# Gate and q/k gain arithmetic moved between VectorE and ScalarE, and a new slot table, in a two-layer mixer and expert-retrieval kernel on one core

## What is computed

```
h = rms(x, g_mix);  x = x + mixer(h)      # 11 projected pieces of 256 columns, four mixers
h = rms(x, g_ffn);  x = x + peer(h)

mixer: qd = rms(heads(dq), g_q_dil) * 64**-0.5 ; kd = rms(heads(dk), g_k_dil)
       qs = rms(heads(bq), g_q_sb)  * 64**-0.5 ; ks = rms(heads(bk), g_k_sb)
       gating, dilated attention, short convolution, stick-breaking attention -> w_out

peer, for each token and each of 8 heads:
       s = two score vectors over 128 keys;  top 16 of each;  top 16 of the 256 sums
       g = softmax(top 16);  a = u_tab[eidx] . h ;  w = g * gelu(a)
       y += sum_k w_k * v_tab[eidx_k]
```

## Time and profile before

| | us | share of the span |
|---|---|---|
| profiled execution, device time | 3106.51 | |
| its span in the profile | 3104.7 | |
| TensorE busy | 2457.8 | 79% |
| VectorE busy | 2307.4 | 74% |
| ScalarE busy | 1421.0 | 46% |
| GpSimd busy (DMA issue) | 1237.1 | 40% |
| gathered by GpSimd's queue | 1073.81 MB | |
| moved in all | 1210.26 MB, mean 390 GB/s | |

### The profile page before, as it was taken

How to read it: one execution, slowest core, us unless ns; L and a number is a source line. 1 busy time by engine, 2 the same in 40 slices (tenths; PEclk the granted TensorE clock), 3 DMA queues, 4 the chain that set the end, 5 groups by cost and what they waited for, 6 DMA issues and landing times. The chain is left out here.

```text
span 3104.7 us, 28006 instructions
## 1 busy us (share of the span) xinstructions
PE 2457.8 (79%) x7696; PEld 1397.8 (45%) x7696; DVE 2307.4 (74%) x5378; ACT 1421.0 (46%) x3800; POOL 1237.1 (40%) x1028
## 2 busy tenths in 40 slices
PE   6579777897676887997787788897889888857666
PEld 5546354563354443663354444573445444322222
DVE  2496769568869998666867899667786899866665
ACT  2144634337643454335643455436683444533332
POOL 0133433333333344434444444334454444445443
PEclk9689889897788899999899998998899999988889
DMA  7399999899789999999999999999999999999998
GB/s 276 122 415 402 421 411 418 324 395 344 292 337 377 358 404 380 422 421 421 415 421 421 390 421 421 421 421 410 367 421 417 421 421 414 422 421 414 422 422 347
DMA packets 169787, 1210.26 MB, mean 390 GB/s; under 512 B 20896, under 2 KB 21152, under 8 KB 23200
## 3 DMA queue, kind: packets, MB, share of 16 engines
q0 software_dynamic: 147456, 1073.81, 84.6%
q1 hardware_dynamic: 22176, 134.66, 10.7%
HBM read 1206.29 MB, written 2.10 MB: 389 GB/s over the span
## 5 line engine op out<-in xcount | busy, mean ns | idle before, releaser
L462 POOL DMA_INDIRECT ring<-in_uv,idx x1024 | 1236.9, 1208 | 1844.5 <-PE psY L811 929.8
L811 PE MATMUL psY<-ring 128*128 128x512 f32 x3120 | 1579.0, 650 | 291.8 <-ACT ring L657 236.4
L1072 DVE CUSTOM_DVE_ANT_0 ring<-ring,htok 128x1024 f32<-128x1024 f32 x1024 | 1234.2, 1221 | 396.0 <-DMA ring<-in_uv,idx 382.0
L811 PEld LDWEIGHTS psY<-ring 128*128 128x128 f32 x3120 | 620.9, 208 | 1051.2 <-issue 1042.0
L647 ACT ACTIVATE gl<-adot 128x1 f32<-128x1 f32 x1024 | 205.1, 200 | 1055.0 <-DVE adot L1072 1032.3
L1083 DVE SCALAR_TENSOR_TENSOR x<-ring,wgt,x 128x1024 f32<-128x1024 f32 x244 | 312.3, 1280 | 24.0 <-issue 24.0
L684 PE MATMUL psP<-hT,wr 128*128 128x256 f32 (+1 forms) x1664 | 322.8, 351 | 3.8 <-ACT hT L499 3.1
L657 ACT ACTIVATE ring<-cst,wgt 128x128 f32<-128x128 f32 x780 | 313.3, 402 | 25.4
L688 PE MATMUL psP<-wr,hT 128*128 128x256 f32 x1344 | 308.0, 385 | 19.0 <-DMA wr<-in_w_out 13.6
L651 ACT ACTIVATE wgt<-gate,gl 128x1 f32<-128x1 f32 x1024 | 301.6, 295 | 33.3
L684 PEld LDWEIGHTS psP<-hT,wr 128*128 128x128 f32 x1664 | 283.8, 200 | 72.8 <-issue 39.3
(11 more groups left out here) (124 smaller groups left out, 1658.7 us busy)
## 6 DMA issues: line engine op xcount, KB each, us to landing
wr<-in_w_in SPq DMA_DIRECT2D x44, 1024.0 KB
wr<-in_w_q SPq DMA_DIRECT2D x40, 1024.0 KB
ring<-in_uv,idx POOLq DMA_INDIRECT x1024
wr<-in_w_out SPq DMA_DIRECT2D x16, 1024.0 KB
ring<-in_w_in SPq DMA_DIRECT2D x11, 1024.0 KB, 17.3
probs<-in_subkeys SPq DMA_DIRECT2D x5, 1024.0 KB
ring<-in_w_out SPq DMA_DIRECT2D x4, 1024.0 KB, 17.1
cat<-in_g_ffn SPq DMA_DIRECT2D x5, 512.0 KB, 12.6
```

The costliest lines, as they stand in the source:

```text
L462: pool.indirect_dma_start(out=ring[:, q % NR], out_offset=None, in_=tables[s // NC], in_offset=bass.IndirectOffsetOnAxis(ap=idx[:, s % NS, ...
L811: last = nc.tensor.matmul(psY[:, b * 512:(b + 1) * 512], ring[:, r % NR, 0:P], ring[:, r % NR, D + b * 512:D + (b + 1) * 512], start=first ...
L1072: v.tensor_tensor_reduce(out=u, in0=u, in1=htok[:, q // SLOTS % NS], scale=1.0, scalar=0.0, op0=ALU.mult, op1=ALU.add, accum_out=adot[:, J ...
```

## The change

Six edits:

- The gate: VectorE no longer subtracts the largest of the 16 (ScalarE negates it into `nmax_top` and gives it to the exponential as a bias), and no longer multiplies by 1/sum (ScalarE does at a head's first row). `top` becomes two buffers `tops`, and "top pairs" waits for the exponential of two heads earlier.
- The q/k gains: ScalarE multiplies by a gain for each partition while it takes the transposes from PSUM. VectorE multiplies q's 8 roots by 1/8 instead of the 512 values. One DMA of a [128, 4] tile takes the place of four broadcast ones.
- The parameters: two semaphores. ScalarE's hT1 waits for three small DMAs (`s_gain`), VectorE waits for the other three (`s_par`) only in the mixer parts of a layer's first step, and no longer in norm1.
- norm2: no copy to `hn`, TensorE transposes `htok`.
- No row is VectorE's in heads 6-7, 16-20, 31-36 and 47-53 (two of 16 before), so 204 rows are left to it.
- The slot table: top_rate of step 1 from 0.95 to 1.10, of (2,3) from 1.2 to 1.3, of (6,7) from 1.5 to 1.55; the three pairs start 3 slots later.

```diff
@@ -47,8 +47,7 @@
-GROUPS = [((0,), -72, 1.0, 1.0), ((1,), 22, 1.0, 0.95), ((2, 3), 126, 0.7, 1.2), ((4, 5), 336, 1.15, 1.3),
-          ((6, 7), 594, 0.97, 1.5)]
+GROUPS = [((0,), -72, 1.00, 1.00), ((1,), 22, 1.00, 1.10), ((2, 3), 129, 0.70, 1.30), ((4, 5), 339, 1.15, 1.30), ((6, 7), 597, 0.97, 1.55)]
 GROUP_LIST = [steps for steps, *_ in GROUPS]
@@ -165,11 +164,14 @@
-    return BUSY_ROWS.get(J, (3, 7, 11, 15))
-
-
-BUSY_ROWS = {J: (1, 3, 5, 7, 9, 11, 13, 15) for J in range(9, 16)}
-BUSY_ROWS.update({J: (7, 15) for lo, hi in ((6, 8), (16, 21), (31, 37), (47, 54)) for J in range(lo, hi)})
+    return BUSY_ROWS.get(J, VR)
+
+
+VR = (3, 7, 11, 15)
+VB = (1, 3, 5, 7, 9, 11, 13, 15)
+VF = ()
+BUSY_ROWS = {J: VB for J in range(9, 16)}
+BUSY_ROWS.update({J: VF for lo, hi in ((6, 8), (16, 21), (31, 37), (47, 54)) for J in range(lo, hi)})
 V_NO, _counts = {}, [0, 0]
@@ -233,7 +235,7 @@
         gain_t = sb("gain_t", [P, 2, KD])
-        g64 = sb("g64", [P, 4, HD])
+        g_col = sb("g_col", [P, 4])
         gsv = sb("gsv", [P, MW])
@@ -276,13 +278,14 @@
         si = sb("si", [P, 2, TOPK], U32)
-        top = sb("top", [P, TOPK])
+        tops = sb("tops", [P, 2, TOPK])
+        nmax_top = sb("nmax_top", [P, 1])
         pos = sb("pos", [P, 3, TOPK], U32)
...
         gsum = sb("gsum", [P, 1])
-        rsum = sb("rsum", [P, 1])
+        rsum = sb("rsum", [P, NS, PH])
         adot = sb("adot", [P, 2, TOPK])
@@ -403,10 +407,11 @@
             def parameters(l):
-                for dst, src in ((gain_t[:, 0], g_mix), (gain_t[:, 1], g_head), (sgb, b_sgu), (cvw, conv_w)):
+                for dst, src in ((gain_t[:, 0], g_mix), (gain_t[:, 1], g_head), (g_col, g_qk)):
+                    sp.dma_start(dst[:], src[l]).then_inc(s_gain, 16)
+                for dst, src in ((sgb, b_sgu), (cvw, conv_w)):
                     sp.dma_start(dst[:], src[l]).then_inc(s_par, 16)
-                for dst, g in ((g64[:, 0], g_qd), (g64[:, 1], g_kd), (g64[:, 2], g_qs), (g64[:, 3], g_ks), (gsv, g_sgu)):
-                    sp.dma_start(dst[:], g[l].partition_broadcast(P)).then_inc(s_par, 16)
+                sp.dma_start(gsv[:], g_sgu[l].partition_broadcast(P)).then_inc(s_par, 16)
@@ -444,7 +449,7 @@
-        N_PAR, N_LATE = 9 * 16, 16
+        N_GAIN, N_PAR, N_LATE = 3 * 16, 3 * 16, 16
@@ -514,7 +519,7 @@
                 elif part == "hT1":
-                    act.wait_ge(s_par, N_PAR * (l + 1))
+                    act.wait_ge(s_gain, N_GAIN * (l + 1))
                     take_hT("hT1", s, 0, 0)
@@ -548,8 +553,9 @@
                         v = psT[:, n % 2].rearrange("p (a b) -> p a b", a=4)
-                        nc.scalar.activation(dq[:, j], v[:, 0:2], ACT.Copy)
-                        nc.scalar.activation(dk[:, :, c * P:(c + 1) * P], v[:, 2:4], ACT.Copy).then_inc(tp_taken, 1)
+                        nc.scalar.activation(dq[:, j], v[:, 0:2], ACT.Copy, scale=g_col[:, 2 * m:2 * m + 1])
+                        nc.scalar.activation(dk[:, :, c * P:(c + 1) * P], v[:, 2:4], ACT.Copy,
+                                             scale=g_col[:, 2 * m + 1:2 * m + 2]).then_inc(tp_taken, 1)
                 elif part == "v squares":
@@ -633,8 +639,10 @@
                         act.wait_ge(gate_ready, T)
-                    g = gate[:, s % NS, i * TOPK:(i + 1) * TOPK]
-                    nc.scalar.activation(g, g, ACT.Exp, accum_out=gsum[:]).then_inc(top_exp, 1)
+                    top = tops[:, T % 2]
+                    link(nc.scalar.activation(nmax_top[:], top[:, 0:1], ACT.Copy, scale=-1.0))
+                    nc.scalar.activation(gate[:, s % NS, i * TOPK:(i + 1) * TOPK], top, ACT.Exp, bias=nmax_top[:],
+                                         accum_out=gsum[:]).then_inc(top_exp, 1)
@@ -647,6 +655,8 @@
                         act.wait_ge(gate_ready, TOP_NO[s, J % PH] + 1)
+                        g = gate[:, s % NS, n:n + TOPK]
+                        link(nc.scalar.activation(g, g, ACT.Copy, scale=rsum[:, s % NS, J % PH:J % PH + 1]))
                     for i in range(NG):
@@ -727,8 +737,9 @@
                     pe.wait_ge(normed, n + 1)
+                    t = htok[:, s % NS] if part == "hT2" else hn
                     for b in range(2):
-                        transposes(BATCH_NO[part, s, 0] + b, [hn[:, (4 * b + k) * P:(4 * b + k + 1) * P] for k in range(4)])
+                        transposes(BATCH_NO[part, s, 0] + b, [t[:, (4 * b + k) * P:(4 * b + k + 1) * P] for k in range(4)])
                 elif part == "piece":
@@ -874,9 +885,9 @@
                 n = NORM_NO.get((part, s), 0) + 1
+                if c == 0 and part in ("conv", "sgu in", "sgu"):
+                    dve.wait_ge(s_par, N_PAR * (l + 1))
                 if part == "norm1":
-                    if c == 0:
-                        dve.wait_ge(s_par, N_PAR * (l + 1))
                     root(n, 1, D)
@@ -884,11 +895,10 @@
                     hv = hn[:].rearrange("p (h d) -> p h d", d=HD)
-                    link(v.tensor_tensor(hv, tmq[:, j].rearrange("p a (h d) -> p (a h) d", d=HD), per_head(rs, 16), ALU.mult))
-                    h4 = hn[:].rearrange("p (a h d) -> p a h d", a=4, d=HD)
-                    link(v.tensor_tensor(h4, h4, g64[:].unsqueeze(2).broadcast_to([P, 4, H, HD]), ALU.mult))
-                    q = hn[:].rearrange("p (a b c) -> p a b c", a=2, b=2)[:, :, 0]
-                    v.tensor_scalar(q, q, HD ** -0.5, None, ALU.mult).then_inc(qk_done, 1)
+                    q = rs[:].rearrange("p (a b h) -> p a b h", a=2, b=2)[:, :, 0]
+                    link(v.tensor_scalar(q, q, HD ** -0.5, None, ALU.mult))
+                    v.tensor_tensor(hv, tmq[:, j].rearrange("p a (h d) -> p (a h) d", d=HD), per_head(rs, 16),
+                                    ALU.mult).then_inc(qk_done, 1)
                 elif part == "bias":
@@ -1005,9 +1015,8 @@
                         dve.wait_ge(gain_in, 16 * (GROUP_LIST.index(GROUP_OF[s]) + 1))
-                    link(v.scalar_tensor_tensor(out=htok[:, s % NS], in0=x[:, c], scalar=rs[:, 0:1], in1=gain_f,
-                                                op0=ALU.mult, op1=ALU.mult))
-                    v.tensor_copy(hn[:], htok[:, s % NS]).then_inc(normed, 1)
+                    v.scalar_tensor_tensor(out=htok[:, s % NS], in0=x[:, c], scalar=rs[:, 0:1], in1=gain_f,
+                                           op0=ALU.mult, op1=ALU.mult).then_inc(normed, 1)
                 elif part == "top keys":
@@ -1021,12 +1030,12 @@
                         dve.wait_ge(vx_used, v_rows(PH * (s - NS + 1), 1))
-                    o = slice(i * TOPK, (i + 1) * TOPK)
+                    T = TOP_NO[s, i]
+                    if T >= 2:
+                        dve.wait_ge(top_exp, T - 1)
                     link(v.tensor_tensor(cand, sv[:, 0].unsqueeze(2).broadcast_to([P, TOPK, TOPK]),
                                          sv[:, 1].unsqueeze(1).broadcast_to([P, TOPK, TOPK]), ALU.add))
-                    found[0] = top16([(cand.rearrange("p a b -> p (a b)"), top, pos[:, 0], sc2)])
-
-                    mark(v.tensor_scalar(gate[:, s % NS, o], top[:], top[:, 0:1], None, ALU.subtract))
+                    found[0] = top16([(cand.rearrange("p a b -> p (a b)"), tops[:, T % 2], pos[:, 0], sc2)])
@@ -1042,9 +1051,7 @@
                     dve.wait_ge(top_exp, TOP_NO[s, i] + 1)
-                    g = gate[:, s % NS, i * TOPK:(i + 1) * TOPK]
-                    link(v.reciprocal(rsum[:], gsum[:]))
-                    v.tensor_scalar(g, g, rsum[:], None, ALU.mult).then_inc(gate_ready, 1)
+                    v.reciprocal(rsum[:, s % NS, i:i + 1], gsum[:]).then_inc(gate_ready, 1)
@@ -1111,8 +1118,8 @@
         "g_ffn": np.asarray(g_ffn_norm),
-        "g_sgu": np.asarray(g_sgu_v), "g_qd": np.asarray(g_q_dil), "g_kd": np.asarray(g_k_dil),
-        "g_qs": np.asarray(g_q_sb), "g_ks": np.asarray(g_k_sb),
+        "g_sgu": np.asarray(g_sgu_v),
+        "g_qk": np.tile(np.stack([np.asarray(g) for g in (g_q_dil, g_k_dil, g_q_sb, g_k_sb)], axis=-1), (1, P // HD, 1)),
         "uv0": np.concatenate([np.asarray(peer_u)[0], np.asarray(peer_v)[0]], axis=1),
...
     }
```

More of the change, by code:

```diff
@@ L215, in trunk @@
 def trunk(nc, x_in, cst_in, w_in, w_out, w_q, subkeys, w_sgu, b_sgu, conv_w, g_mix, g_head, g_ffn,
-          g_sgu, g_qd, g_kd, g_qs, g_ks, *rest):
+          g_sgu, g_qk, *rest):
     tables, out = rest[:DEPTH], rest[DEPTH]
@@ L301, in trunk @@
         s_x = [sem(f"s_x{c}") for c in range(NC)]
+        s_gain = sem("gain_t_loaded")
         s_par = sem("params_loaded")
```

## The result

The changed kernel takes 3067.9 us (median of 4 runs, 3066.4 to 3072.5), the kernel before 3104.2 beside it. The ratio is 0.9889, with a 95% interval of 0.9876 to 0.9901, so 31 to 38 us less. The forecast was 3080, in a range of 3062 to 3098.

The account below looks back on a forecast made before the run. Only 230 us in which the DMA engines had too little to do could be won, with VectorE setting the pace in 950:1250. Terms -9.5 - 15 - 3 + 2 + 1 = -24.5 us gave 3080, range 3062 to 3098.

Parts of the forecast that it names:

- A, the start: Before the first row: TensorE starts 7.4 us earlier without VectorE's wait, plus 1.25, 0.7 and 0.1: 9.5 us won.
- The upper bound for the three small loads: At the start: if ScalarE's small loads took until 12.0 us, the start's gain would shrink to about 4 us.
- B, the choice of keys for (2,3): Stretch 950:1250, where VectorE sets the pace: relieving it wins 15 of 26 us, bounds 0 and 26.
- the sum in which VectorE needs 30.2 us against the DMA's 29.4: Per pair of heads of (2,3): VectorE goes from 103% to 91% of the DMA's time, slots from 10.8 to 11.7.
- C, the rest: Same relief for (4,5) and (6,7), where the DMA is mostly full, and norm2's copies: 3 us won, bounds 0 and 10.
- The 79 us lost in 550:950: Front of (2,3) at tight rate 0.7: the DMA loses 79 us to parts that wait for each other in order.
- D, ScalarE: Gate on ScalarE: negation takes the wait, the table load comes after the indices; 2 us lost, bounds 0 and 10.
- E, later indices: Pairs start 3 slots later; GpSimd's wait for (6,7) grows to 12.3 us, just covered: 1 us lost, bounds 0 and 12.
- F, layer two: First norm1 of layer two: VectorE's 10.75 us wait for parameters goes, worth nothing since weights were loading meanwhile.
- TensorE did not become the bound: Rival, chance 0.08: TensorE bounds heads without VectorE rows, deciding from 2.0 us a row; 3159 us.
- Only the start: Rival, chance 0.18: stretch 950:1250 is held by the order of parts, not VectorE's amount of work; 3097 us.
- All of the loss of 950:1250 goes: Rival, chance 0.10: all 26 us of that stretch won, with 10 us for the later pairs; 3062 us.

Follow-up runs that it names:

- start_only: The kernel before with only the parameter semaphores split, the four broadcast gain tiles still loaded: 3103.5 us, ratio 0.9990.
- slots_rates: The kernel before with the three new top_rates and the old start slots: 3095.4 us, ratio 0.9970.
- gate_dve: The changed kernel with the gate arithmetic back on VectorE, slot table and V rows as changed: 3057.6 us, ratio 0.9845.
- only_qk_norm2_start: The kernel before with only the start, q/k gains and norm2 as changed; slot table, V rows and gate arithmetic as before: 3092.4 us, ratio 0.9964.
- early_load: The changed kernel with one more ScalarE exponential, of a constant column, ahead of the wait for the indices: 3060.8 us, ratio 0.9861.
- both_old: The changed kernel with the slot table and the V rows of the kernel before: 3113.9 us, ratio 1.0021.

## Why the prediction was right or wrong

**The time** lay in the range, 12 us below the forecast, and the side was right. The parts were right less often than the sum.

**A, the start: right.** 9.5 us forecast, 8.8 us at head 0 and 9.4 in GpSimd's first wait. The upper bound for the three small loads (12.0 us) did not occur: ScalarE's take of the transposes at 10.92 waited for TensorE and not for them. The rule of the Trainium skill, DMA: Bandwidth & Descriptors, Specifications, was put against this edit for its loads under 512 bytes. The three that `s_gain` counts cost nothing here, since they had landed before anything needed them. What did cost were the four further ones, broadcast, of 256 bytes a partition, which the rule covers as well: with them in the queue the weights were waited for 5.51 us in start_only. The working named that effect as a help and gave it no price; it is 3.8 of the 6.9 us. So the 7.4 us put down to the semaphore were 3.1 of the semaphore's and 3.8 of the loads', and the forecast came out because both were changed.

**B, the choice of keys for (2,3): the size right, the cause wrong, so the size is luck.** 15 us forecast, 16 us found in heads 15 to 24. But the step that failed is the sum in which VectorE needs 30.2 us against the DMA's 29.4, and afterwards 28.9 against 31.6: it counts all three ways of easing VectorE alike. The V rows did help, 8 to 9 us over the whole kernel in either slot table. The gate work taken off VectorE did not: the move cost 14 us in the new table and 18 in the old one. The slot table was by far the largest, 29 us alone and 32 on top of the rest, and not by the 11.7 slots for 10.8 that the sum has: this widening without the later starts won 0.3 us in these heads (slots_rates). VectorE at 91% was a symptom that two causes can give: too much work, and waits between short pieces of work. gate_dve shows that its amount of work alone does not decide: more VectorE work, and fewer us. The two signs that the prediction named for B, VectorE under 90% (251 of 282 us, 89%) and 400 GB/s or more (404), both came true and could not tell the causes apart.

**C, the rest: too small, and outside its bounds.** 3 us forecast, bounds 0 and 10; heads 5 to 15 alone gave 11 to 14. The step that failed is the choice of what "the rest" is. I looked at (4,5) and (6,7), where the DMA is mostly full, and left out step 1's choice of keys, in heads 5 to 8, which was also spread (0.95 to 1.10, 6 us by itself). The 79 us lost in 550:950 were put down to the front's own tight rate, which didn't change, and mostly they did stay: from the first dot product at the front's first slot to that at its last, 113 rows on, it is 399.7 us before and 394.3 after.

**D, ScalarE: the mechanism right, the size too small by a factor of seven to nine.** It named the negation that takes the wait, and the load behind it; the timeline shows just that. I took 2 us of bounds 0 and 10. It is 14 to 18, outside the bounds. The step that failed is "the row loop has ten buffers, so one delay of 1.5 is covered": the covered path was the row's, and the path that was not covered is the next head's scores, whose copy stands behind the gates on ScalarE and for which VectorE then stands still with everything in its own queue: a wait of 89.9 us with the load exposed, 45.9 with it hidden, 36.7 without the gate move. The Trainium skill, ScalarE: Activation LUTs, Rules for kernel authors, says to multiply on VectorE; for the gate the runs agree, 14 us for it. The reason the page gives is VectorE's speed for each element; what was found here, for some 9 of the 14, is the load's place in ScalarE's queue. The q/k gains went to ScalarE as well, into copies that it made anyway, and only_qk_norm2_start, which has them, lost nothing after the start. By the Trainium skill, ScalarE: Activation LUTs, What ACT_TABLE_LOAD costs, a switch is 2.66 us with its drain; here the negation ends at 1191.49, the load starts at 1191.51 and the exponential at 1192.81, 1.30 us after it, so the drain does not show and is not the reason.

**E, later indices: right as far as can be told.** 1 us forecast of bounds 0 and 12; none measured for two of the three pairs, to within some 6 us. The wait itself was over-sized: 12.3 us forecast ahead of row 768, 7.7 found.

**F, layer two: held.** VectorE's first norm1 of layer two no longer waits for the parameters:

```profile
1215.12 0.16 DVE L851 TENSOR_SCALAR nt<-ss 128x1 f32<-128x1 f32 x1 [1.56 <-ACTq L492]
```

1.56 us for ScalarE's sum of squares in place of 10.75. That this was worth nothing fits start_only, which drops the same wait of VectorE: it is 3.3 us ahead of the kernel before at head 20 and 2.4 at head 24.

**The rivals.** TensorE did not become the bound. Rows on it in the changed kernel's choice of keys:

```profile
1079.34 7.03 PE L822 MATMUL psY<-ring 128*128 128x512 f32 x16
...
1086.20 0.61 PE L803 MATMUL psS<-probs,qdsT 128*128 128x128 f32 x4
```

Sixteen records, four rows, until the next work in 1086.20 - 1079.34 = 6.9 us, 1.72 a row as before, far from the 2.0 from which it would decide. *Only the start* (3097) was wrong for the change as a whole; what is left when the table, the V rows and the gate move are all undone is 11 us. *All of the loss of 950:1250 goes* (3062) was the nearest in time; the rate there rose to 404 GB/s and not to 421.

So that the sum came near is luck, since two errors stood against each other: B and C together had 18 us for everything that eases the choice of keys, where the table alone is worth 29 to 32 and the V rows 8 to 9, and D had 2 us for the gate move, where it costs 14 to 18. The best version here is gate_dve at 3057.6 us (3055.8 with the old starts of the last pairs, the same within the interval).

## What to carry to other kernels

When several engines run fixed queues, ask of an instruction put ahead of a wait, or in place of the one that waited, what used to happen inside that wait; here a table load inside the wait cost nothing, and the same load behind it some 9 us. An engine at 91% need not be short of time: look at what it waits for between its pieces before taking work off it. And where a hand-written table sets the order, price each of its numbers like an instruction, and together as well as one by one, for here six numbers were worth more than all the instructions moved, and more than the sum of their parts.

## What the runs showed of the hardware

- The place of the table load: 1.28 us in 62 of 64 heads, behind the wait, were worth some 9 us of the whole, give or take 6 (changed kernel against early_load); an exponential of a constant column ahead of the wait brings them back.
- Broadcast loads of small tiles were dear to what was queued behind them: with four of 256 bytes a partition in the queue the first weights were waited for until 17.18 us, without them until 13.33. In 6:12 the DMA engines moved 36 GB/s with them and 258 without; 1.4 of the 3.8 us are the time in which SyncE issued three more loads.
- No time beyond the load itself showed at a change of the table: the exponential started 1.30 us after the start of a load of 1.28 (both_old).
